# Order of the high and low weight products in the feed-forward up and gate products

## The reference

```
n = rmsnorm(h, g_ffn[l])
h = h + (jax.nn.silu(n @ w_gate[l]) * (n @ w_up[l])) @ w_down[l]
```

## Time and profile before

| what | value |
|---|---|
| time, median of 3 runs | 747.33 us (746.35 to 747.41) |
| span of the profiled execution | 745.2 us |
| TensorE busy | 740.4 us, 99% |
| VectorE busy | 518.0 us, 70% |
| ScalarE busy | 416.4 us, 56% |
| products of L1592, 704 | 179.2 us |
| products of L1597, 704 | 98.8 us |
| weights and inputs read | 128.68 MB, 175 GB/s over the span |

### The profile page before, as it was taken

The page is one execution under the profiler, slowest core; times in us unless marked ns, Lnnn a source line. Parts: engine busy times, 40 slices in busy tenths (PEclk is TensorE's granted clock), DMA queues, the critical chain, the costliest instruction groups (busy, mean ns, idle before and its releaser), DMA issues.

```text
span 745.2 us, 11582 instructions
## 1 busy us (share of the span) xinstructions
PE 740.4 (99%) x4563; PEld 641.4 (86%) x4563; DVE 518.0 (70%) x834; ACT 416.4 (56%) x788; POOL 66.5 (9%) x103
## 2 busy tenths in 40 slices
PE   9999999999999999999999999999999999999998
PEld 8999999877888888888888888887888888888886
DVE  5784677885756678887367757898667777447762
ACT  5575557556463455565356546597646656345640
POOL 6300000000010000430000004400100000000000
PEclk9999999999999999999999999999999999999999
DMA  8998444343455546766656461735355655656611
GB/s 266 297 311 274 85 109 153 114 128 123 146 170 197 167 152 222 198 213 228 188 172 212 171 226 54 251 124 174 111 168 170 191 204 174 222 170 188 207 57 56
DMA packets 99209, 131.26 MB, mean 176 GB/s; under 512 B 5357, under 2 KB 79163, under 8 KB 99156
## 3 DMA queue, kind: packets, MB, share of 16 engines
q1 hardware_dynamic: 96564, 125.58, 52.6%
q0 software_dynamic: 2304, 4.43, 2.7%
q10 hardware_dynamic: 288, 0.52, 0.2%
HBM read 128.68 MB, written 1.84 MB: 175 GB/s over the span
## 4 chain that ended last, share of the span: by engine, by line
PE 97%; DVE 2%; ACT 1%; issue 0%; POOL 0%; POOLq 0%
PE B L1626 39%; PE B L1592 22%; PE B L1597 11%; PE B L1581 11%; PE B L1805 2%; PE B L1852 2%; PE B L1815 2%; PE B L1639 1%; PE B L1685 1%; PE B L1633 1%; DVE LO L1002 1%; PE B L1808 1%; PE B L1832 1%; PE B L1730 1%; PE B L1791 0%; PE B L1729 0%
## 5 line engine op out<-in xcount | busy, mean ns | idle before, releaser
L1002 DVE TENSOR_TENSOR LO<-RAW,HI 128x1024 fp32r<-128x1024 f32 x236 | 282.5, 1236 | 101.0 <-ACT HI L538 100.5
L1626 PE MATMUL B<-HI,AA 128*128 128x512 f32 (+1 forms) x960 | 286.8, 376 | 0.3 <-DVE AA L1008 0.2
L538 ACT ACTIVATE HI<-RAW 128x1024 fp32r<-128x1024 f32 (+1 forms) x240 | 237.2, 1038 | 63.1 <-PE B L1626 58.2
L1626 PEld LDWEIGHTS B<-HI,AA 128*128 128x128 f32 x960 | 175.7, 188 | 33.8 <-issue 1.6
L1592 PE MATMUL B<-AA,HI 128*128 128x512 f32 x704 | 179.2, 393 | 0.0
L1626 PE MATMUL B<-LO,AA 128*128 128x512 f32 (+1 forms) x480 | 178.6, 372 | 0.0
L1592 PEld LDWEIGHTS B<-AA,HI 128*128 128x128 f32 x704 | 126.8, 189 | 23.0 <-issue 0.7
L1626 PEld LDWEIGHTS B<-LO,AA 128*128 128x128 f32 x480 | 90.6, 189 | 14.6
L1597 PEld LDWEIGHTS B<-AA,LO 128*128 128x128 f32 x704 | 96.6, 190 | 7.1
L1597 PE MATMUL B<-AA,LO 128*128 128x256 f32 x704 | 98.8, 282 | 0.0
L1581 PE MATMUL B<-AA,HI 128*128 128x256 f32 x448 | 83.3, 287 | 0.0
(11 more groups left out here) (313 smaller groups left out, 634.9 us busy)
## 6 DMA issues: line engine op xcount, KB each, us to landing
RAW<-in_w_in SPq DMA_DIRECT2D x29, 1024.0 KB, 5.8
RAW<-in_w_gate SPq DMA_DIRECT2D x22, 1024.0 KB, 5.3
RAW<-in_w_up SPq DMA_DIRECT2D x22, 1024.0 KB, 5.3
RAW<-in_w_down SPq DMA_DIRECT2D x22, 1024.0 KB, 5.0
RAW<-in_w_in SPq DMA_DIRECT2D x10, 512.0 KB, 6.4
RAW<-in_w_attn_out SPq DMA_DIRECT2D x4, 1024.0 KB, 5.1
RAW<-in_w_o SPq DMA_DIRECT2D x4, 1024.0 KB, 5.0
RAW<-in_w_out SPq DMA_DIRECT2D x4, 1024.0 KB, 5.0
```

The lines of the kernel that those rows point to most:

```text
L538: e.activation(pieces(HI, NSPL, i, k), pieces(RAW, NRAW, i, k), ACT.Copy).then_inc(split_hi, 1)
L1002: e.tensor_tensor(pieces(LO, NSPL, i, k), pieces(RAW, NRAW, i, k), pieces(HI, NSPL, i, k), ALU.subtract).then_inc(split_lo, 1)
L1626: x = e.matmul(dst, a, w[:, t, c0:c0 + n], start=(first and t == 0 and k == 0), stop=(last and t == nk - 1 and k == 2))
```

## The change

`both` gets another order where `part` is not 1. `low` now makes a single product, and the body runs over `t`: high 0, then low 0, high 1, low 1, and so on, up to high 6, low 6, low 7, high 7. The last high remains the last instruction of the group, and the first remains the first. `part=1` has the same instructions in the same order as before. Instructions, operands, waits and semaphores are the same in number and kind; what waits stood ahead of a group stand ahead of it still. No other engine's list changes. In the new file the low product stands at L1596, and the lines behind it move by six.

```diff
@@ -1592,23 +1592,29 @@
                     return e.matmul(dst[:, :], hi[:, t, c0:c0 + 128], flatten(AA[:, ch + t, :, :]), start=(t == 0),
                                     stop=(t == nk - 1))
 
-                def low():
-                    for t in chunks(nk, part):
-                        e.matmul(dst[:, 0:S], lo[:, t, c0:c0 + 128], AH[:, ch + t, :], start=False, stop=False)
+                def low(t):
+                    e.matmul(dst[:, 0:S], lo[:, t, c0:c0 + 128], AH[:, ch + t, :], start=False, stop=False)
 
                 if new:
                     unit_ready(i, 0 if part == 0 else 1)
                 if part == 1:
                     if when:
                         e.wait_ge(when[0], when[2])
-                    low()
+                    for t in chunks(nk, part):
+                        low(t)
                 if when:
                     e.wait_ge(when[1], when[2])
-                for t in chunks(nk, part)[:-1]:
-                    high(t)
-                if part != 1:
-                    low()
-                return high(chunks(nk, part)[-1])
+                if part == 1:
+                    for t in chunks(nk, part):
+                        x = high(t)
+                    return x
+                x = high(0)
+                for t in chunks(nk, part)[1:]:
+                    low(t - 1)
+                    if t == chunks(nk, part)[-1]:
+                        low(t)
+                    x = high(t)
+                return x
 
             def moving(i, c0, n, dst, ch, tt, new, first=True, last=True, when=None, part=None):
```

## The result

The changed kernel is slower: 748.97 us in the median of seven runs (748.57 to 749.79), against 746.72 (746.09 to 747.41) for seven runs of the kernel before beside them. The ratio is 1.0029, with a 95% interval of 1.002 to 1.0039. That is 2.2 us more, where 747.1 was forecast from a base of 747.33, which is a change of -0.2 us. The time lies inside the stated range, but the direction is wrong: the forecast said "no change", and what came is the price of the slow rival (2820 ns for a group, +2.5 us).

What follows compares the result with a forecast made beforehand. TensorE, busy 740.4 of 745.2 us, was taken as the bound. 589 + 6 x 230 + 7 x 117 = 2788 ns a group against 2790, times 84 groups: -0.2 us, so 747.1 us from 747.33; range 743.6 to 750.9.

Steps and rivals of the forecast that it cites:

- the slow rival: At L1592, each high behind a low costs 233 ns, each low 119: 2820 a group, 749.8 us; chance 0.28.
- What bounds the kernel: TensorE is busy 740.4 of 745.2 us, so nothing stands between a change in its pace and the end.
- That the neighbour matters: In TensorE's groups, changing from lows to highs costs, not the highs: 227 ns settled, 233 and 236 behind lows.
- (a): Parts of a group that don't alternate: last high 233, next group's first high 236, eighth low 120; together 589 ns.
- (b): Six highs in a group that each follow a single low: 230 ns each, the middle of 227 and 233.
- (c): Seven lows in a group that each follow a single high: 117 ns each, between 115 and 119.
- The settled sum: Eight highs at 227 and eight lows at 120 ns: 2776 ns a group, with a group before 14 above.
- the rival in which the order does nothing: Each product in a group costs its settled price whatever its neighbour: 2776 ns, 1.2 us less, 746.1 us; chance 0.12.
- (d): Four `part=0` groups, with two lone lows and two highs behind them: at most 0.1 us either way, taken as nothing.
- (e): Supply to TensorE from VectorE and ScalarE: ten us in 55.80 are free, so no new wait; cost nothing.
- The rule of the Trainium skill: Gap of columns / 2.4 + 2.5 ns: high 216, low 109 in any order; zero change, 747.3 us.

Runs made afterwards that it cites:

- the row of patterns: Kernel before with about 700 unread products appended on TensorE in patterns of 24 pairs; whole time means nothing; high and low in turn took 353 ns a pair.
- four H LL with HHHH: Whole groups ordered high, two lows, four times, then four highs, against the kernel before: 748.42 against 747.00 us, ratio 1.0022; also repeated as an appended pattern.
- the twelve orders of a group: Kernel before with about 1,600 unread products appended: twelve orders of eight highs and eight lows, each repeated eight times; whole time means nothing; 2786.7 to 2820.0 ns a group.

## Why the prediction was wrong

- **What bounds the kernel: right.** TensorE alone set the end, its waits stayed the same, and what a group gained or lost came out in the time, in both directions and within the intervals, in all the kernels above but the one that joined four groups everywhere.
- **That the neighbour matters: right.** The excess of a group over its settled sum is due to the going from lows to highs; joining two groups halved it.
- **(a), what does not alternate: right.** 589 forecast; after, the first and the last high and the eighth low take 234.6, 234.5 and 119.5, 589 together, in the mean of the settled groups.
- **(b), six highs behind single lows: wrong, and this is the step that failed.** I took 230, the middle between 227 and 233, "since one low has had an eighth of the time to unsettle what eight lows unsettle". After, the six take 235.3 in the mean of the settled groups (224 to 241). 6 x 5.3 = 32 ns, which is all by which the group missed. The picture behind it, of one price that goes by how long the lows before have been, is wrong. The alternation has two steady forms. In the cheap one highs take 230 and lows 117, just as forecast, and the third group of each network takes the forecast 2788 ns; but no later group is in it. And in the row of patterns the highs of an alternation take 235, 232, 241, over and over, and a high can cost more there (241) than behind sixteen lows (236 at most). The nearest row in shape was the lone high of the earlier trace rows, with 233 for itself and 119 for its low. It would have given 2820 ns to the nanosecond, in part by luck: its 233 is 2 too low for a high and its 119 is 2 too high for a low, and the errors cancel. I had called it the nearest, and then took a middle with an end that no row of an alternation supported.
- **(c), seven lows behind single highs: right in size.** 117 forecast, 117 measured. Of its two ends one was misread: a low behind settled highs takes 113 by the starts and not 115, since the offset of 162 to 163 ns between duration and distance does not hold there (278 - 113 = 165). The middle would have been 116.
- **The settled sum.** 2776 came from rounded distances; it is 2773, and a group of before lies 20 ns above it, not 14. No term of the sum uses it, only the rival in which the order does nothing.
- **(d): nothing, as taken.** The four `part=0` groups don't show in the sum.
- **(e), supply: right for this change, and narrower than it looked.** Joining four groups moved TensorE's demand for banks, not the amount of work, and cost 2.0 us of waits.
- **The slow rival** had the place and the price: "TensorE never settles", 2820 ns, with 233 + 119 = 352 ns a pair; measured are 235 + 117 in the group, and 353 in steady alternation. The threshold it named, 348 a pair, was passed. Its reason, several highs in a row needed to settle, does not hold up: the cheapest order of a single group has never more than two highs in a row, and the alternation itself also ran at 347 a pair.
- **The rule of the Trainium skill** ("TensorE: Matmul & The Clock Gate", Back-to-back issue gap) gives each product a gap by its own columns. By it this change would have cost nothing. No run here agrees: the same 16 products take 2778 to 2820 ns by order alone.

So the change is slower because in 78 of its 84 whole groups a high and its low take 352 ns in the mean and not 347. That is shown. Why 512 and 256 columns in turn have a dear and a cheap form, and what picks one, stays open.

## What to carry to other kernels

Where TensorE is busy 99% of the time, the order of equal work is worth tenths of a per cent either way, and it is read best from start-to-start distances; counts and shares of busy time look the same. Of the orders here, long runs of one width that neighbouring groups share were the cheapest (2784 and 2778 ns), then two and two (2787), as long as each bank is free again when it is asked for. Before a finer order goes into a kernel, append it as a repeated pattern behind the last product and read its steady distance: that row gave 2793, 2820 and 2787, and the kernels gave the same. But a pattern can have two steady forms. The row gave 2807 or 2820 for one sequence, and the kernel ran both, so read the kernel's own stretches too.

## What the runs showed of the hardware

- A product of n columns with 128 x 128 weights of four bytes takes n / 2.4 + 13.3 ns from start to start in a long run of its kind at the full granted clock (2.4 GHz); the formula is fitted to four widths: 120.0 for 256, 146.7 for 320, 173.3 for 384, 226.7 for 512. Others lie beside it: 480 columns took 216.5 instead of 213, 448 took 202 instead of 200, 288 took 132 instead of 133.
- In turns, widths don't always add up: 512 with 256 costs 6.7 ns a pair too much, 384 with 256 nothing, 352 with 256 even 6.7 too little, and 512 with 128 takes 340 ns. Another bank, the other half of the bank, and a high part in place of the low one changed nothing, to the nanosecond.
- One sequence of products can have two steady forms: 512 and 256 in turn 347 and 353 ns a pair, 512 and 384 in turn 406 and 413, and four H LL with HHHH 2807 and 2820 ns a group.
- The steady sums of ten of the twelve orders of a group are multiples of 6.67 ns above each other (2786.7, 2793.3, 2806.7, 2820.0); the other two, 2797 and 2798, are means over unlike groups. This looks like products starting at fixed beats, with patterns that fit them well or badly; that is a guess, and no run shows the beat itself.
- Lighter weights (120, 96, 32 columns) made runs of 512 columns slower (230 to 233 instead of 226.7), in one run of 24 products each.
